# Second attention: its joins on GpSimd, values as the stationary operand, gates laid out by feature, and half of the turned-weight copies on VectorE

## What is computed

```python
def _stick_breaking(q, k, v):
    ...
        mask = kpos[None, :] < qpos[:, None]
        z = jnp.einsum('bhqd,bshd->bhqs', qb, k).astype(jnp.float32) * scale
        log_beta = jax.nn.log_sigmoid(z)
        log_1mb = jnp.where(mask, jax.nn.log_sigmoid(-z), 0.0)
        suffix = lax.cumsum(log_1mb, axis=3, reverse=True) - log_1mb
        a = jnp.where(mask, jnp.exp(log_beta + suffix), 0.0)
        return jnp.einsum('bhqs,bshe->bhqe', a.astype(v.dtype), v)

def _sb_layer(x, k, v, norm_g, w_in, w_out):
    proj = _rms(x, norm_g) @ w_in
    q, g = jnp.split(proj, [SB_W], axis=-1)
    o = _stick_breaking(q.reshape(b, s, SB_HEADS, SB_HEAD_DIM), k, v)
    o = o.reshape(b, s, SB_W) * jax.nn.silu(g)
    return x + o @ w_out
```

## Time and profile before

| | us |
|---|---|
| median of 3 runs | 2390.4 |
| lowest, highest | 2380.78, 2392.75 |
| the profiled execution | 2385.55 |
| its span in the trace | 2383.7 |
| PE busy in the span | 2301.2 |
| DVE busy | 1592.2 |
| ACT busy | 1017.9 |
| POOL busy | 208.1 |
| first scan of the last attention | 1980.75 from the start |
| first output product | 2284.33 from the start |

### The profile page before, as it was taken

How to read it: one execution, slowest core, us unless ns; L and a number is a source line. 1 busy time by engine, 2 the same in 40 slices (tenths; PEclk the granted TensorE clock), 3 DMA queues, 4 the chain that set the end, 5 groups by cost and what they waited for, 6 DMA issues and landing times.

```text
span 2383.7 us, 30315 instructions
## 1 busy us (share of the span) xinstructions
PE 2301.2 (97%) x12762; PEld 1234.2 (52%) x12762; DVE 1592.2 (67%) x2053; ACT 1017.9 (43%) x1482; POOL 208.1 (9%) x254
## 2 busy tenths in 40 slices
PE   7999999999999999999999988999999999989999
PEld 5445444444444444445544456654444446777765
DVE  6888867866766666787632389965534406989961
ACT  6255334322323223433322587732313216888841
POOL 0001030000000001623301100022000000000000
PEclk9999999999999999999999999999999999999999
DMA  5111010111110212103111000111231200010021
GB/s 187 36 37 69 1 36 36 61 46 71 58 49 36 71 71 71 38 1 142 36 71 36 32 5 1 62 46 36 71 141 36 72 1 1 1 36 1 1 89 54
DMA packets 50488, 116.02 MB, mean 49 GB/s; under 512 B 2418, under 2 KB 8107, under 8 KB 49968
## 3 DMA queue, kind: packets, MB, share of 16 engines
q1 hardware_dynamic: 48616, 105.40, 12.4%
q10 hardware_dynamic: 1736, 8.68, 0.9%
HBM read 101.49 MB, written 12.58 MB: 48 GB/s over the span
## 4 chain that ended last, share of the span: by engine, by line
PE 80%; DVE 11%; ACT 6%; issue 1%; DMA 1%; SPq 0%; DVEq 0%; ACTq 0%
PE PS L72 76%; PE PS L75 4%; ACT RG L81 3%; DVE R L93 2%; DVE RG L107 2%; ACT OV L84 2%; DVE R L101 1%; DVE RG L104 1%; DVE RG L101 1%; DVE RG L93 1%; ACT R L81 1%; DMA RG<-in_a_w_in 1%; DVE oss L110 1%; DVE dg L104 1%; DVE scl L110 0%
## 5 line engine op out<-in xcount | busy, mean ns | idle before, releaser
L72 PE MATMUL PS<-R,RG 128*128 128x512 f16 (+1 forms) x5184 | 1104.2, 374 | 9.4 <-DVE R L101 4.2
L72 PEld LDWEIGHTS PS<-R,RG 128*128 128x128 f16 (+1 forms) x5184 | 514.0, 104 | 592.8 <-issue 10.9
L72 PE MATMUL PS<-RG,R 128*128 128x512 f16 (+1 forms) x2904 | 631.2, 377 | 2.0 <-DVE R L101 1.7
L72 PEld LDWEIGHTS PS<-RG,R 128*128 128x128 f16 x2904 | 283.7, 98 | 330.0 <-issue 2.9
L81 ACT ACTIVATE RG<-RG,scl 128x4096 f16<-128x4096 f32 (+2 forms) x70 | 177.9, 2557 | 199.5 <-DVE scl L113 199.5
L101 DVE SCALAR_TENSOR_TENSOR RG<-RG,scl 128x4096 f16<-128x4096 f32 (+2 forms) x70 | 213.1, 3051 | 71.5 <-ACT RG L81 71.5
L101 DVE SCALAR_TENSOR_TENSOR R<-PS,scl,R 128x512 f32<-128x512 f32 (+1 forms) x227 | 159.2, 742 | 121.2 <-PE PS L72 98.8
L81 ACT ACTIVATE R<-PS,scl 128x512 f32<-128x512 f32 (+1 forms) x128 | 83.5, 685 | 326.4 <-PE PS L72 287.0
L107 DVE TENSOR_TENSOR_SCAN RG<-RG 128x127 f32<-128x127 f32 (+7 forms) x128 | 168.4, 1343 | 76.3 <-ACT RG L81 76.1
L110 DVE TENSOR_REDUCE scl<-RG 128x1 f32<-128x4096 f32 (+1 forms) x35 | 150.3, 4293 | 98.9 <-DMA RG<-in_w_ff 41.1
L72 PE MATMUL PS<-R,OV 128*128 128x64 f32 (+2 forms) x1456 | 193.7, 274 | 5.7 <-DVE R L93 5.4
(11 more groups left out here) (137 smaller groups left out, 1667.2 us busy)
## 6 DMA issues: line engine op xcount, KB each, us to landing
RG<-in_w_ff SPq DMA_DIRECT2D x16, 2048.0 KB, 8.5
RG<-in_a_w_in SPq DMA_DIRECT2D x8, 2048.0 KB, 8.7
xspill<-R ACTq DMA_DIRECT2D x2, 4096.0 KB, 16.0
RG<-in_w_kv SPq DMA_DIRECT2D x4, 2048.0 KB, 8.2
RG<-in_b_w_in SPq DMA_DIRECT2D x4, 2048.0 KB, 8.1
RG<-in_w_in SPq DMA_DIRECT2D x3, 2048.0 KB, 8.2
R<-in_x SPq DMA_DIRECT2D x8, 512.0 KB, 8.0
RG<-in_w_out SPq DMA_DIRECT2D x2, 2048.0 KB, 7.8
```

The source lines that it names most:

```text
L72: return self.engine.matmul(*a, **k) if self.engine else Nothing()
```

## The change

- **Joins on POOL.** The 86 `tensor_tensor` of step 4 leave DVE's queue for POOL's. They now wait for `scanned` (DVE) and `beta` (ACT). POOL's 8 `across` of the gates go.
- **Second copies on DVE.** Of step 5, ACT keeps the first half (up to 512 columns); DVE copies the second (`turned_second`), as a `tensor_copy` from PSUM, in step u for group u-2, just before the scan of u.
- **Values stationary.** In step 6 a 128 x 64 block of values is the stationary operand and 128 columns of turned weights are moving. The output has 64 features on partitions 0 to 63 or 64 to 127, by the head's parity.
- **Gates by feature.** Tiles 38 and 39 go through `product_t`; the gate lies in GT (RG 8192 to 12287 and R0). No `gate_turn`: `gate_high` and `gate_low` read the gated values from SBUF. A bound of their size comes from a matmul with ones over the sums of token blocks 0 to 6 (`gate_bound(0, 7)`), and one for block 7. The splitting of blocks 0 and 1 moves to step u = N of the attention's loops (N = 86), on DVE ahead of the last group's second copy.
- **Places.** EB is `eb(u)` (RG 0 to 2047 for two groups, then four buffers at 4096); tile 40 goes to slot 1, is loaded a second time after group 1 is turned, and its pieces move to groups 26 to 33. The output rows lie in R2, the split gated values in R3.

```diff
-            return i % 3 if i < 40 else i - 40
+            return i % 3 if i < 40 else 41 - i
...
-        sb_pieces = range(22, 30)
+        sb_pieces = range(26, 34)
...
-            for t in range(NT - 1):
-                for c in range(2):
-                    product_n(38 + c, t, ("g2", t, c), bank=6 + c if t == NT - 2 else None)
...
+            for z, key in enumerate(G2[:14]):
+                _, c, mi, n = key
+                product_t(38 + c, mi, n, h_rhs, key, bank=z - 6 if z >= 12 else None)
...
+                e.matmul(b[:, first:last], ones[:, :], col(24 + first, last - first), start=True,
+                         stop=True).then_inc(*full.up(*key))
...
-                            e.wait_ge(*sig("turned_b").at(v, at // 512))
-                            mm = e.matmul(banks.ap(("pvb", i, g))[:, 64 * (h % 8):64 * (h % 8) + 64],
-                                          AT2[v % 2][:, at:at + 128], V2[:, j, 64 * h:64 * h + 64],
-                                          start=(j == 0), stop=(j == i))
+                            e.wait_ge(*sig("turned_b_dve" if at >= 512 else "turned_b").at(v, at // 512))
+                            r, q = 64 * (h % 2), 128 * (h % 8 // 2)
+                            mm = e.matmul(banks.ap(("pvb", i, g))[r:r + 64, q:q + 128], V2[:, j, 64 * h:64 * h + 64],
+                                          AT2[v % 2][:, at:at + 128], start=(j == 0), stop=(j == i))
...
-            gate_turn(0)
-            gate_turn(1)
...
-                    if c == 0 and t + 2 < NT:
-                        gate_turn(t + 2)
...
+            def turned_second(v):
+                if 0 <= v < N and len(sb_halves(v)) > 1:
+                    s, at, n = sb_halves(v)[1]
+                    e.wait_ge(*full.at("tb", v, s))
+                    if v >= 2:
+                        e.wait_ge(*full.at("pvb", sb_groups[v - 2][0], sb_groups[v - 2][1][-1]))
+                    e.tensor_copy(AT2[v % 2][:, at:at + n], banks.ap(("tb", v, s))[:, 0:n]).then_inc(
+                        *banks.empty([("tb", v, s)], sig("turned_b_dve"), v, s))
...
+                if u > 3:
+                    turned_second(u - 2)
...
-                    scan.then_inc(*step.up())
-                if u < N:
-                    i, hs = sb_groups[u]
-                    w = width(i)
-                    eb, ec = by_head(EB[u % 4], u)[:, :, 0:w - 1], by_head(kept(u), u)[:, :, 1:w]
-                    e.wait_ge(*sig("beta").at(u))
-                    e.wait_ge(*step.last())
-                    e.tensor_tensor(eb, eb, ec, ALU.mult).then_inc(*sig("joined_b").up(u))
+                    scan.then_inc(*sig("scanned").up(u))
...
+                if u == N:
+                    gate_factors(0, 7)
+                    gate_low(0)
+                    gate_low(1)
...
+                if u == N:
+                    gate_high(0)
+                    gate_high(1)
...
-            for i in range(NT):
-                e.wait_ge(*sig("g_peak").at(i))
-                across(col(32 + i), col(24 + i)).then_inc(*sig("g_top").up(i))
+            for u, (i, hs) in enumerate(sb_groups):
+                w = width(i)
+                beta, left = by_head(eb(u), u)[:, :, 0:w - 1], by_head(kept(u), u)[:, :, 1:w]
+                e.wait_ge(*sig("scanned").at(u))
+                e.wait_ge(*sig("beta").at(u))
+                e.tensor_tensor(beta, beta, left, ALU.mult).then_inc(*sig("joined_b").up(u))
...
+            e.wait_ge(*sig("bank_full").at("tb", 1, 1))
+            e.dma_start(w_raw(40).rearrange("p (k n) -> p k n", k=8), w_source(40)).then_inc(
+                *sig("raw_again").up(by=16))
+            load(41)
```

More of the change, by code:

```diff
@@ L557, in product_t, with product_n @@
                 last_product[i] = key
-            def product_n(i, t, key, ready=None, bank=None):
+            def product_n(i, t, key, ready=None, bank=None, lhs=h_lhs):
                 b = banks.take(key) if bank is None else banks.take_at(key, bank)
@@ L1014, in tensor, with gate_bound @@
                     product_t(36 + c, mi, n, h_rhs, ("q2", c, mi, n), ready=h_ready("b_norm_2", n))
-            for t in range(NT - 1):
-                for c in range(2):
-                    product_n(38 + c, t, ("g2", t, c), bank=6 + c if t == NT - 2 else None)
-            def gate_turn(i):
-                for g in range(2):
-                    b = banks.take(("gt", i, g))
-                    e.wait_ge(*sig("g_gated").at(i, g))
-                    e.wait_ge(*banks.free(("gt", i, g)))
-                    for k in range(4):
-                        at = 512 * g + 128 * k
-                        mm = e.transpose(b[:, 128 * k:128 * k + 128], GG[:, i, at:at + 128], ident[:, :])
-                    mm.then_inc(*full.up("gt", i, g))
+            for z, key in enumerate(G2[:14]):
+                _, c, mi, n = key
+                product_t(38 + c, mi, n, h_rhs, key, bank=z - 6 if z >= 12 else None)
+            def gate_bound(first, last, bank):
+                key = ("gate_bound", first)
+                b = banks.take_at(key, bank)
+                e.wait_ge(*sig("g_peak").at(last - 1))
+                e.wait_ge(*banks.free(key))
+                e.matmul(b[:, first:last], ones[:, :], col(24 + first, last - first), start=True,
+                         stop=True).then_inc(*full.up(*key))
             e.wait_ge(*sig("constants").at("mask_s"))
@@ L2063, in gate_low, with gate_factors @@
             def gate_low(i):
+                e.wait_ge(*sig("g_high").at(i, 1))
                 for g in range(2):
[L2065 to L2073 removed]
+                    up = sig("g_low").up(i) if g else step.up()
+                    low_half(HG[:, i, g, 0, :, :], HG[:, i, g, 1, :, :], gated_at(i, g), col(40 + i)).then_inc(*up)
+            def gate_factors(first, last):
+                key, n = ("gate_bound", first), last - first
+                e.wait_ge(*full.at(*key))
+                power(col(63 + first, n), col(40 + first, n), banks.ap(key)[:, first:last], key=key).then_inc(
+                    *sig("g_factor").up(first))
             N = len(sb_groups)
@@ L2118, in vector @@
                         *(sig("weight").up(40) if u - 1 == sb_pieces[-1] else step.up()))
-            for i in range(2):
-                gate_factor(i)
-                gate_low(i)
+                if u == N:
+                    gate_factors(0, 7)
+                    gate_low(0)
+                    gate_low(1)
             for c in range(2):
```

129 lines of the change are left out of this document (65 added, 64 removed).

## The result

The changed kernel takes 2418.96 us (median of 4 runs, 2416.73 to 2419.51) against 2390.66 for the kernel before: a ratio of 1.0125, 95% interval 1.0096 to 1.0154, or +28 us where +41.5 was forecast (against the medians of the kernel before in the three later sets, 2386.3 to 2388.2, it would be 31 to 33). The profiled run has a span of 2414.9 us, 31.2 more than before.

What follows compares the result with a forecast made beforehand. It took DVE and PE alike to bound the last attention, and scans and joins excluding each other after the change. +49.5 - 1 - 7 = +41.5 on the median 2390.4 gave 2432 us, range 2402 to 2480.

Steps and rivals of the forecast that it cites:

- Exclusion: In the last attention a scan and a POOL join can't overlap, having two SBUF inputs each; stage 344 us, chance 0.74.
- Rival 1: In the last attention a scan doesn't shut POOL out: 2382 us, not slower; chance 0.14.
- The price of a join: A join on POOL costs 2.13 ns a column and 0.17 us an instruction: 171 us in place of 90.4.
- the sign "near 2325": If the forecast is right, the last join of the last attention ends near 2325 us.
- Part 3: Values as stationary operand in the last attention: doubling the moving columns costs nothing measurable, taken as 0.
- Rival 2: PE becomes the bound of the last attention, by slower loads and changes of array shape: 2475 us; chance 0.12.
- +49.5 for the stage: Last attention, first scan to last join: 168.4 + 171 - 3 + 6 + 2 = 344 us, before 294.9.
- Second copies on DVE: In the last attention, 86 copies from PSUM, between 24 and 59 us in all, run beside the joins and cost nothing.
- The end: After the last join: -1 us up to the first output product, -7 us over seven intervals of output products.

Runs made afterwards that it cites:

- e_scan_psum: The changed kernel with the scan's unused second input read from PSUM in place of SBUF, which adds waits: 2426.1 us, ratio 1.0163.
- e_copies_act: The changed kernel with the second copies back on ACT, joins still on POOL: 2413.1 us, ratio 1.0113.
- e_end: The changed kernel with joins on DVE, second copies on ACT, sigmoids of groups 2 and 3 moved, block 7's gate bound two output blocks later: 2390.8 us.
- e_joins_only: The kernel before with only its joins moved to POOL, POOL's gate reductions coming behind them: 2433.2 us, ratio 1.0173.
- parts 3 and 4 alone: The changed kernel with the joins back on DVE and the second copies back on ACT: 2393.6 us, ratio 1.0031.

## Why the prediction came near

The forecast was 2432 us, and 2419 came. By the traces the change costs 42.8 - 0.7 - 5.6 = 36.5 us, where the sum had 41.5; the other 8 us of the 13 come from no term of the change: 5.3 are the earlier start of the attention in the profiled run, the rest is between profiled runs and medians. That the sum came within 5 us of the traces is partly luck, as follows.

**Exclusion: right.** The prediction took the scan to shut POOL out as other instructions with two SBUF inputs did. Its signs came true: joins start as scans end, scans that meet a join take 2.47 to 3.85 us with 1024 keys, most of them 2.94 or 3.40, and scan and join add up to the step. e_scan_psum shows that the second SBUF input is the reason. Rival 1 (a free scan, 2382 us) fell.

**The price of a join: mis-sized.** The sum had 2.35 us for 1024 columns, 171 us in all, from two POOL instructions of another kind, the one of 1024 columns with an operand in PB, the one of 512 within R. The joins, whose operands both lie in RG, took 2.00 us for 1023 columns and 1.32 for 639: (2.00 - 1.32) / 384 = 1.77 ns a column. In all they took 149.8 us, with 3.4 in it for the eight that met a low half of tile 40, where the sum had 6 us apart. That is 21 us less, and the step 4.22 in place of 4.63. The last join ended at 2313.2, 338 us after the first scan, in place of 344; the sign "near 2325" missed by 12 us.

**Values stationary: the step that failed.** Part 3 was taken as 0, on the grounds that 128 moving columns cost no more than 64. That ground holds (3.75 against 3.72 us a step), but the term left out what the same paragraph mentioned, the changes of shape. They are 13.2 us of stage with the joins on DVE and 6.7 in the changed kernel. Rival 2 named them and priced a step at 5.1 us: 16 x 0.05 for the instructions, which is wrong (0.142 - 0.129 = 0.013 each), and 4 x 0.2, which is near to the 4 x 0.17 seen. PE's step came to 3.95, just under the exclusion's 4.22, so the rival did not decide, and yet was not free.

**What lay around scans and joins.** The sum took scans and joins (339.4) and 5 us more. Before, the stage had 294.9 - 258.8 = 36 us of other things on DVE and idle time, and the prediction let nearly all of it vanish under the exclusion. Of the changed kernel's 337.7 us, 168.4 + 149.8 = 318.2 are scans and joins, and 19.5 are not. Some 6.7 of these are the changes of shape, 1.3 the wait at the start, 3.3 the second copies (by e_copies_act's stage), each from one pair of profiled runs; the rest, some 8 us, isn't split further. Part of it lies in the first groups, where DVE waits 4.35 and 3.43 us for PE at two gate products between joins 3 and 4. So +49.5 for the stage was nearly right at +42.8 because -21 and about +15 stood against each other, and that is luck.

**Second copies on DVE: right in size, not in reason.** They hide beside the joins with many keys, as forecast. In the first groups they don't (12.7 in place of 8.4 us between two joins). The times can't tell the difference from 0.

**The end: right.** -1 and -7 were forecast, -0.7 and -5.6 came. The missing 1.4 us is PE's wait for the bound of block 7's gates (7.06 between the first two products), which the prediction passed over; e_end takes it away.

**The parts don't add.** With 1024 keys a step grows from 3.72 us by 0.50 with part 1 alone (the nine even steps of e_joins_only) and by 0.22 with parts 3 and 4 alone, but with all three (e_copies_act) by 0.54 and not 0.72. DVE with POOL (4.22 us a step) and PE (3.95) are bounds side by side, and the larger one counts. Over the whole stage part 1 alone is +48.0, but with an unknown part for the clock, parts 3 and 4 alone are +19.8, and all with part 2 are +42.8. The direct consequence: undoing the joins on POOL, and the second copies with them, leaves a kernel that is still slower than before by 0.31%, though by the prediction it should have been 8 us faster.

## What to carry to other kernels

In this kernel work moved from VectorE to GpSimd ran in parallel with VectorE's copies from PSUM and with scans that read one input from SBUF, and not with those that read two: look at the operands of both, name by name, before counting the gain, and see whether an input that is not used can come from elsewhere without adding a wait. When the stationary operand of a matrix product changes its width, price the change of the array's shape at each switch, not the columns. And where two resources are near the bound in one stage, a sum for one of them must be set beside the other's new sum; a change that breaks both costs the larger, and undoing one part shows the other.

## What the runs showed of the hardware that was not expected

- A scan blocked by a POOL join ends 2.13 or 2.14 us after it, with 2.28 us of its own, however much of the join it met: it does not advance while it is blocked. In the other order a join of 2.00 us ends 1.78 us after the scan. The same scan with its second input in PSUM took 2.28 us, so PSUM costs it no time.
- POOL's two-input multiplication depends on what its operands are: 2.00 us for 1023 columns in one area, 2.35 for 1024 with an operand in PB. The 1.26 us for 512 columns within R is also over the joins' line, 1.10 by 1.77 ns a column and 0.19 us. Which property makes the difference was not tried.
- A change between 128 x 128 and 128 x 64 leaves 0.17 us of idle weight loads each way; the one from 64 x 128 to 128 x 128, behind the scores, stays at 0.42.
- In e_joins_only waits of PE of 1.37 to 2.53 us, in a stage that otherwise keeps it busy, were followed by stretches at 1.2 GHz (0.50 granted), in which eight products took 1.81 in place of 1.00 us. Such waits did not always bring it: the changed kernel has four of 1.34 to 1.47 us from 2190 on without a fall, and one stretch at the lower level behind a wait of 1.73 us at 1994. Which kernels fall into this and how often was not predictable from their steps.
